# One decoder layer, 32 experts from a ring of slots: expert 3's gate instead of expert 28's in spare memory, and a queue that loads one expert ahead

## The reference

```
logits = xt @ w_router + b_router;  top 4 of 32;  combine = softmax over the four, as a (256 x 32) matrix
for each expert e of 32:
    g = min(xt @ w_gate[e] + b_gate[e], 7);   u = clip(xt @ w_up[e] + b_up[e], -7, 7)
    y = ((u + 1) * g * sigmoid(1.702 * g)) @ w_down[e] + b_down[e]
    acc += combine[:, e] * y
x = x + acc
```

## Time and profile before

| | us |
|---|---|
| median of 3 runs | 1132.2 |
| profiled execution | 1131.85 |
| its span, first to last instruction | 1129.9 |
| TensorE busy (matmul) | 1073.4 (95%) |
| VectorE, ScalarE, GpSimd busy | 452.4, 170.7, 90.1 |
| loads: 440.09 MB, mean over the span | 389 GB/s |

### The profile page before, as it was taken

One profiled execution on the slowest core, in us unless ns is written; L12 is line 12 of the kernel. 1 busy time (PEld: TensorE's weight loads), 2 busy tenths in 40 slices (PEclk: granted clock), 3 DMA queues, 4 the chain that ended last, 5 costly groups with the idle time before them and its releaser, 6 DMA issues.

```text
span 1129.9 us, 14464 instructions
## 1 busy us (share of the span) xinstructions
PE 1073.4 (95%) x5719; PEld 510.5 (45%) x5719; DVE 452.4 (40%) x1070; ACT 170.7 (15%) x342; POOL 90.1 (8%) x89
## 2 busy tenths in 40 slices
PE   9999999999999998989889999999899999899998
PEld 7779899843333333333333333333333333233333
DVE  5883666533333333333333333333333233333333
ACT  7546655300000000000000000000000000000000
POOL 3227446000000000000000000000000000000000
PEclk9999999999999999999999999999999999999999
DMA  9836424999999999999999999999999999999996
GB/s 382 361 149 253 195 76 171 421 422 430 427 431 429 432 434 428 432 432 435 427 429 432 430 433 426 431 431 427 431 431 430 427 431 429 431 427 428 427 423 259
DMA packets 27536, 440.09 MB, mean 389 GB/s; under 512 B 3009, under 2 KB 4418, under 8 KB 6114
## 3 DMA queue, kind: packets, MB, share of 16 engines
q1 hardware_dynamic: 26752, 438.71, 91.5%
q10 hardware_dynamic: 738, 0.73, 0.2%
HBM read 438.38 MB, written 1.05 MB: 389 GB/s over the span
## 4 chain that ended last, share of the span: by engine, by line
PE 67%; DMA 30%; DVE 1%; ACT 1%; issue 0%; POOL 0%; DVEq 0%; POOLq 0%
PE bank L1936 40%; DMA ring<-in_w_e_up_dram 30%; PE bank L1901 3%; PE bank L1958 2%; PE bank L1691 1%; PE bank L1921 1%; PE bank L1692 1%; PE bank L1693 1%; PE bank L1980 1%; PE bank L1536 1%; PE bank L1960 1%; PE bank L1778 1%; PE bank L1545 1%; PE bank L1737 1%; PE bank L1779 1%; PE bank L1780 1%
## 5 line engine op out<-in xcount | busy, mean ns | idle before, releaser
L1936 PE MATMUL bank<-ring,heads 128*64 128x512 f32 x3004 | 690.8, 606 | 0.2 <-DVE heads L1335 0.2
L1936 PEld LDWEIGHTS bank<-ring,heads 128*64 128x64 f32 x3004 | 204.0, 138 | 388.4 <-issue 387.8
L1474 DVE TENSOR_TENSOR x<-x,bank 128x512 f32<-128x512 f32 x124 | 79.6, 683 | 145.9 <-PE bank L1960 145.9
L925 ACT ACTIVATE heads<-heads 128x512 f32<-128x512 f32 x32 | 20.2, 630 | 669.6 <-DVE heads L1407 669.6
L1444 DVE SCALAR_TENSOR_TENSOR y_lo<-bank,small,y_hi 128x512 fp32r<-128x512 f32 x31 | 23.3, 750 | 212.5 <-ACT y_hi L921 212.5
L1921 PE MATMUL bank<-bias_parts,e_sel 128*128 128x512 f32 x63 | 32.6, 518 | 46.4 <-DMA ring<-in_w_e_up_dram 42.8
L728 POOL TENSOR_TENSOR x<-x,heads 128x256 f32<-128x256 f32 x2 | 1.4, 726 | 907.7 <-ACT heads L947 907.7
L397 POOL TENSOR_TENSOR w_lo<-ring,w_hi 128x1024 fp32r<-128x1024 f32 (+1 forms) x35 | 65.3, 1890 | 53.6 <-ACT w_hi L751 53.6
L1901 PEld LDWEIGHTS bank<-work,xn 128*128 128x128 f32 x480 | 55.9, 192 | 12.2 <-issue 12.2
L751 ACT ACTIVATE w_hi<-ring 128x512 fp32r<-128x512 f32 (+2 forms) x82 | 57.1, 731 | 23.2 <-PE bank L1780 7.4
L1901 PE MATMUL bank<-work,xn 128*128 128x128 f32 x480 | 60.0, 278 | 0.0
(11 more groups left out here) (315 smaller groups left out, 1030.6 us busy)
## 6 DMA issues: line engine op xcount, KB each, us to landing
ring<-in_w_e_down_dram SPq DMA_DIRECT2D x58, 2048.0 KB, 23.8
ring<-in_w_e_gate_dram SPq DMA_DIRECT2D x24, 4096.0 KB, 28.5
ring<-in_w_e_up_dram SPq DMA_DIRECT2D x24, 4096.0 KB, 31.1
ring<-in_w_e_gate_dram SPq DMA_DIRECT2D x13, 2048.0 KB, 19.4
ring<-in_w_e_up_dram SPq DMA_DIRECT2D x13, 2048.0 KB, 19.3
ring<-in_w_e_down_dram SPq DMA_DIRECT2D x12, 1024.0 KB, 24.0
ring<-in_w_merge_dram SPq DMA_DIRECT2D x4, 2048.0 KB, 8.6
spare<-in_w_e_gate_dram SPq DMA_DIRECT2D x1, 4096.0 KB, 17.9
```

The costliest lines, as they stand in the source:

```text
L1474: ins = nc.vector.tensor_tensor(x[:, t, 512 * h:512 * h + 512], x[:, t, 512 * h:512 * h + 512], bank67[:, j % 2, :], ALU.add)
L1936: last = mm(bank[C * half:C * half + C, :], lhs(kk), kept_row[half] if kept else w[:, k, 512 * half:512 * half + 512], start=(kk == 0 and ...
```

## The change

The `gate` in `spare` is expert 3's. It is used in the fourth step, and expert 28's `gate` is loaded through the ring by the loop. In the ring every load from `down` 2 on comes one place earlier, so the first loads get a table of places (`FIRST_PLACE`) and `PAIR_ORDER` is turned by one, which leaves the loads of experts 0 to 2 in the slots that they had. The loop's body for step `it` now issues `gate` of it + 1, `down` of `it` and `up` of it + 1 (before: `gate` of `it`, `down` of it - 1, `up` of `it`); `first_experts` also issues `gate` 4, `down` 3 and `up` 4; the last group has three turns of loads instead of four.

```diff
-PAIR_ORDER = (3, 2, 1, 0)
+PAIR_ORDER = (0, 3, 2, 1)
+        FIRST_PLACE = {("gate", 0): 1, ("up", 0): 2, ("gate", 1): 3, ("down", 0): 4, ("up", 1): 5, ("gate", 2): 6,
+                       ("down", 1): 7, ("up", 2): 8, ("down", 2): 9, ("up", 3): 10}
+        IN_SPARE = ("gate", STEPS - 1)
...
             def load_spares():
                 sp.wait_ge(proj_done, 12)
-                sp.dma_start(spare[...], a[ex_src["gate"]][E - STEPS]).then_inc(spare_in, 16)
+                sp.dma_start(spare[...], a[ex_src["gate"]][IN_SPARE[1]]).then_inc(spare_in, 16)
...
                 as_freed("down", 1, "gate", 2)
                 as_freed("up", 2, "down", 1)
-                as_freed("gate", 3, "up", 2)
-                as_freed("down", 2, "gate", 3)
-                as_freed("up", 3, "down", 2)
+                as_freed("down", 2, "up", 2)
+                as_freed("up", 3, "gate", 3)
+                sp.wait_ge(mat_done["down"], 2)
+                load_matrix("gate", STEPS, place_of("gate", STEPS))
+                for h in range(2):
+                    sp.wait_ge((half_done, mat_done)[h]["up"], 3)
+                    load_half("down", h, STEPS - 1, place_of("down", STEPS - 1))
+                sp.wait_ge(mat_done["down"], 3)
+                load_matrix("up", STEPS, place_of("up", STEPS))
...
-                sp.wait_ge(mat_done["up"], prev)
-                load_matrix("gate", e, place_of("gate", u))
-                sp.wait_ge(mat_done["gate"], now)
+                e_next = sp.snap(sp.to_reg((it + 1) & (E - 1)), min_val=0, max_val=E - 1)
+                now, following = sp.to_reg(it), sp.to_reg(it + 1)
+                sp.wait_ge(mat_done["up"], now)
+                load_matrix("gate", e_next, place_of("gate", u + 1))
+                sp.wait_ge(mat_done["gate"], following)
                 for h in range(2):
-                    load_half("down", h, e_before, place_of("down", u - 1))
-                sp.wait_ge(mat_done["down"], prev)
-                load_matrix("up", e, place_of("up", u))
+                    load_half("down", h, e, place_of("down", u))
+                sp.wait_ge(mat_done["down"], now)
+                load_matrix("up", e_next, place_of("up", u + 1))
...
-            for u in range(STEPS):
+            for u in range(1, STEPS):
                 expert_body(last_base, u, True)
...
-                n = 0 if first and m == "gate" else place_of(m, u)
+                in_first = isinstance(base, int)
+                n = FIRST_PLACE.get((m, u)) if in_first else place_of(m, u)
                 if in_last:
                     n = LAST_PLACE.get((m, u), n)
-                if in_last and (m, u) == ("gate", 0):
+                if in_first and (m, u) == IN_SPARE:
                     pe.wait_ge(spare_in, 16)
                     w = spare[:, h, :].rearrange("p (k n) -> p k n", k=4)
                 else:
                     s = slots_of(n)[h]
-                    halves = isinstance(base, int) or m == "down" or in_last
+                    halves = in_first or m == "down" or (in_last and n not in (-1, 1))
```

More of the change, by code:

```diff
@@ L415, in adds @@
         def adds(n):
-            if n == place_of("down", 0):
+            if n == 0:
+                return 0, 0
+            if n == FIRST_PLACE["down", 0]:
                 return 32, 32
@@ L428, in count_at @@
             if in_last:
-                landed += 16 * (n // 4 + 1)
+                landed += 16 * (n // 4 + 1 + (n % 4 == 3) - (h == 1 and n % 4 in (1, 3)))
             return landed + base * (PER_GROUP[h] // STEPS)
@@ L497, in load_matrix @@
                 s = slots_of(n)[0]
-                src = a[ex_src[m]][bass.ds(e, 1)].rearrange("o p n -> p (o n)")
+                src = a[ex_src[m]][bass.ds(e, 1)] if not isinstance(e, int) else a[ex_src[m]][e:e + 1]
+                src = src.rearrange("o p n -> p (o n)")
                 sp.dma_start(ring[:, s:s + 2, :].rearrange("p s n -> p (s n)"), src).then_inc(ring_in[s], 16)
@@ L517, in load_by_halves @@
                     sp.wait_ge(last_half, 1)
-                    load_part("down", h, 0, place_of("down", 0), 0)
+                    load_part("down", h, 0, FIRST_PLACE["down", 0], 0)
                 for h in range(2):
                     sp.wait_ge(out_done, 2)
-                    load_part("down", h, 0, place_of("down", 0), 1)
+                    load_part("down", h, 0, FIRST_PLACE["down", 0], 1)
             def load_as_used(i):
@@ L535, in load_spares @@
                 sp.wait_ge(proj_done, 12)
-                sp.dma_start(spare[:, :, :].rearrange("p h n -> p (h n)"), a[ex_src["gate"]][E - STEPS]).then_inc(spare_in, 16)
+                sp.dma_start(spare[:, :, :].rearrange("p h n -> p (h n)"), a[ex_src["gate"]][IN_SPARE[1]]).then_inc(spare_in, 16)
             def first_experts():
@@ L543, in as_freed @@
                         sp.wait_ge((half_done, mat_done)[h][of], done)
-                        load_half(m, h, e, place_of(m, e))
+                        load_half(m, h, e, FIRST_PLACE[m, e])
                 sp.wait_ge(*low_done(OUT))
-                load_half("gate", 1, 1, place_of("gate", 1))
+                load_half("gate", 1, 1, FIRST_PLACE["gate", 1])
                 sp.wait_ge(y_made, KD)
-                load_half("gate", 0, 0, 0)
+                load_half("gate", 0, 0, FIRST_PLACE["gate", 0])
                 sp.wait_ge(*low_done(OUT + 3))
                 sp.wait_ge(*low_done(OUT + 4))
-                load_half("up", 0, 0, place_of("up", 0))
+                load_half("up", 0, 0, FIRST_PLACE["up", 0])
                 sp.wait_ge(*low_done(OUT + 7))
                 sp.wait_ge(*low_done(OUT + 8))
-                load_half("up", 1, 0, place_of("up", 0))
+                load_half("up", 1, 0, FIRST_PLACE["up", 0])
                 load_by_halves()
-                load_half("gate", 0, 1, place_of("gate", 1))
+                load_half("gate", 0, 1, FIRST_PLACE["gate", 1])
                 for i in range(len(INTO_USED)):
@@ L571, in expert_body @@
                 e = sp.snap(sp.to_reg(it & (E - 1)), min_val=0, max_val=E - 1)
-                e_before = sp.snap(sp.to_reg((it - 1) & (E - 1)), min_val=0, max_val=E - 1)
-                now, prev = sp.to_reg(it), sp.to_reg(it - 1)
                 if last:
[L575 to L578, removed]
+                    e_before = sp.snap(sp.to_reg((it - 1) & (E - 1)), min_val=0, max_val=E - 1)
+                    now, prev = sp.to_reg(it), sp.to_reg(it - 1)
+                    for h in range(2):
+                        sp.wait_ge((half_done, mat_done)[h]["up"], prev)
+                        load_half("gate", h, e, place_of("gate", u))
                     if ends:
@@ L610, in _ @@
                     sp.wait_ge(turned, N_UNITS)
-                    load_half("gate", 1, 0, 0)
+                    load_half("gate", 1, 0, FIRST_PLACE["gate", 0])
                 if name == "cv1":
```

6 lines of the change are left out of this document (3 added, 3 removed).

## The result

The kernel after takes 1136.55 us (median of 7 runs, 1135.98 to 1137.59), the kernel before beside it 1132.39. The ratio on record is 1.0032, 95% interval 1.0022 to 1.0042 (the quotient of the two medians is 1.0037): slower by 0.2 to 0.4%. The profiled execution has a span of 1134.1 us, 4.2 more than before. The forecast itself, 1135.0, foresaw 2.8 of the 4.2 us. The 1136.55 lie inside the whole range that I gave, 1131.8 to 1137.2, which takes in the rivals, but 1 us above the range of the forecast's own mechanism, 1134.2 to 1135.5.

A forecast was written before the change was run, and what follows sets the result against it. The stream of expert matrix loads was taken to bound the kernel from about 388 us: a 4.4 us pause, a 3.9 us lag and a 2.8 us later end gave span 1132.7 and median 1135.0 us; whole range 1131.8 to 1137.2.

The forecast's parts named there:

- the forecast's own mechanism: At `up` 4 the load stream runs dry for 4.4 us; lag 3.1 to 4.3 us, end 2.0 to 3.2 later; chance 0.60.
- The four loads behind `gate` 3: `up` 3, `gate` 4 and `down` 3 move up by one matrix, landing at 288.8, 298.6 and 308.4 us.
- a second pause behind the first: Sign of being wrong: after the dip, another pause at `gate` 5 or `down` 4, whose cover is 0.4 and 0.1 us.
- the clock rival: At the end, a half-clock stretch doubles the last sixteen matmuls' 1.9 us: 1.9 on top, 1136.9 us; chance 0.10.
- the lag of the stream: From `up` 5 on, every landing is 3.9 us later than the same stream position before; the last at 1123.7 us.
- the 2 MB load: Alone on the engines it took 8.1 us; with 4.9 for another half, 13.0 us was forecast for `up` 4 from rest.
- 0.4 us of cover: At `gate` 5, released 318.8: landing forecast at 332.2 us, where from rest it would be 331.8.
- two late landings of the kernel before: `up` 4 and `up` 5 landed 0.4 and 0.8 us late before; the first was taken as absorbed, the second as recurring.
- no pause: Rival: `down` 2's slot comes free by 305.1 us, so the stream flows through; 1131.0 us; chance 0.12.
- Cheap start: Rival: `up` 4 from rest takes 9.7 us instead of 13.0; pause 1.1, lag 0.6, time 1131.7 us; chance 0.18.
- the Trainium skill's rule: A DMA takes about 2.0 us plus bytes over 436 GB/s: 4 MB in 11.6 us, sum 1133.6; not adopted.
- at most every second long wait: Between 388 and 1000 us: eleven half-clock stretches of 3.3 us were estimated beside 21 TensorE waits of up to 3.4 us.

The follow-up runs named there:

- e1: Against the kernel before: spare memory holds expert 16's gate, its ring slot stays empty, and gate 28 comes through the ring by halves; 1131.5 us, ratio 0.9986.
- e4: Kernel before with one early wait more: SyncE enters the loop only when expert 3's gate has been used; 1140.66 us, ratio 1.0071.
- e5: Kernel before with one wait in the middle: the load of expert 16's gate waits until the gate of 15 has been used; 1132.65 us, ratio 0.9998.
- e7: Kernel after with every matrix loaded by halves, each half released when the same half in its slot has been used; 1136.54 us, ratio 1.0024 to the kernel before.
- e3: Expert 3's gate in spare memory, but its slot kept empty and the kernel before's places and releases kept; gate 28 by halves through the ring; 1140.32 us, ratio 1.0063.
- e6: Kernel after with up 4 in two halves, the first issued once down 2's first half has been used; 1135.86 us, ratio 1.0025 to the kernel before.
- e8: Kernel after with every matrix loaded by halves, both released only when the whole matrix in the slot has been used; 1140.67 us, ratio 1.0050 to the kernel before.
- e10: e1 with down loaded whole in the loop instead of by halves, 24 times; 1130.37 us, ratio 0.9974 to the kernel before.
- e11: Kernel before with down loaded whole in the loop instead of by halves, spare memory as before; ratio 0.9994.

## Why the prediction was right, and by what it was too small

These steps came out as forecast. Bytes and TensorE's work are unchanged. The four loads behind `gate` 3 take over releases and landings (298.6 and 308.4 forecast, 298.6 and 308.6 measured). `up` 4 is issued at 309.7 (309.5 forecast), with no release before. The stream stands still there, and nothing of it is regained later. In the tail TensorE follows the stream directly and gives back 1.0 us (5.2 us of late landing became 4.1 at the last matmuls; 1.1 forecast). e1 shows that the end itself costs nothing, e4 that such a pause costs its length at least, e5 that it needs an uncovered queue, e7 that a sooner release removes most of it.

One thing came that I had named as a sign of being wrong: a second pause behind the first, at `gate` 5. The mechanism of the first holds without it, but the second is not in the sum, and its 1.9 us are more than the 1.3 us by which the lag was forecast too small. As a number 1136.55 is nearer to the clock rival's 1136.9 than to my 1135.0; it is the trace that decides between them, below.

The term that was mis-sized is the lag of the stream: forecast 3.9 us, measured 5.2. It was wrong both ways. A 4 MB load from rest took 12.2 us, not the 13.0 that I built from the 2 MB load, so the pause was 3.6 instead of 4.4. But I wrote for `gate` 5 that it had "0.4 us of cover" and let it follow at 9.7: it came 11.6 behind. I had added the latency from rest to the time of issue and taken that as the floor under any load. With 3.0 us of other loads ahead, `gate` 5 took 14.6, more than from rest. The same is seen elsewhere: 14.1 us with 1.8 ahead (e3), 13.3 from rest 0.6 us after the last landing (e6), 12.4 and 12.2 from rest. A whole matrix with 5.3 us ahead (`gate` 4 in the kernel after, issued at 283.6) came 9.7 us behind its predecessor and lost nothing.

Put together, `gate` 5 is 0.2 (`down` 3 was late already) + 3.6 (the pause) + 1.9 (its own loss) - 0.4 (the load at the same place of the kernel before, `up` 4, was late too) = 5.3 us late. Of the two late landings of the kernel before I let one be absorbed. Both came again in other places (10.1 us at `up` 5, 10.7 at `up` 6), so nothing of them was absorbed for good. Such single late landings, 0.3 to 1.7 us, occur in every one of the profiled kernels, also with 6.6 us and more ahead, and no run shows their cause. A part of the 1.9 us at `gate` 5 may be of that kind; the 2.6 us at `gate` 4 in e3 and the 2.9 in e8 are larger than any of them.

Of the rivals, no pause is refuted by 0 GB/s from 308 to 310 us. Cheap start has a small truth, 12.2 instead of 13.0. The estimate from the Trainium skill's rule (DMA: Bandwidth & Descriptors, "Anatomy of one DMA", fitted on GpSimd's path) is 11.6 us for this load, nearer than my 13.0. For 2 MB the same rule gives 6.8, where the traces have 8.1 and, a few us after other loads, 7.1 and 7.2. For a load with little ahead, such as `gate` 5, it says nothing. The clock took no part in the tail: the last three groups of sixteen take 1.95, 1.89 and 1.88 us. Elsewhere it was there more often than I had written ("at most every second long wait"): in the kernel before, eight of the twelve waits of TensorE over 2 us were followed by a stretch at 1.2 GHz.

## What to carry to other kernels

Where loads are the bound, look for the one place where the load queue has least ahead of it and ask what an edit does to the release there. A matrix kept aside helped here by its full transfer only in the middle of the stream, where the queue is deep (0.0089 of the time, 10.1 us), and by half of that where the consumer still sets the releases (0.0043). So put such a buffer where its turn comes after the queue has filled. It is not enough that the stream is not empty when a load is issued: here a whole matrix with 5.3 us of other loads ahead lost nothing, and whole matrices with 3.0 and 1.8 us ahead lost 1.9 and 2.6 us; no run tried the values between. Compare a change of grain (halves, whole) with its own control, since the grain has a price of its own.

## What the runs showed of the hardware

- Two 4 MB loads that were issued with 1.8 and 3.0 us of other loads ahead took longer to land (14.1 us in e3, 14.6 in the kernel after) than those issued to idle engines (12.2, 12.4 and, in e6, 13.3). For 2 MB it was 10.6 us with 2.8 ahead in e8, and 7.1 and 7.2 from rest in e3 and e8. But 2 MB with 2.3 ahead in e6 took 7.2 and landed at the normal distance, although the rate fell there too (380 GB/s from 307 to 313 us). In the kernel after and in e8 the load in front had itself started from rest, in e3 it had not; what makes the difference stays open.
- In the dip at `gate` 5 the load engines were less idle than slow: from 320 to 326 us they were busy 0.91 of the time, at 347 GB/s in place of 429.
- Two 2 MB loads take 9.78 us in a full stream and one 4 MB load 9.71. Over 24 matrices whole loads brought the last landing 1.9 us forward (e10 against e1) and 1.3 us (e11 against the kernel before).
